# A hybrid decoder trunk in float32: the first half layer's conditioning is made in four column groups, with the first projection pass worked between them

## The reference

```python
cond = jax.nn.silu(c)
for l in range(DEPTH):
    ada = (cond @ w_ada[l] + b_ada[l])[:, None, :]
    sh_m, sc_m, g_m, sh_f, sc_f, g_f = jnp.split(ada, N_ADA, axis=-1)
    h = x * (1.0 + sc_m) + sh_m
    y = hybrid_mixer(h, ...)                      # h @ w_in (2048 x 6672), three head groups, @ w_out
    x = layer_norm(DEEPNORM_ALPHA * x + (1.0 + g_m) * y, ln_g[l, 0], ln_b[l, 0])
    h = x * (1.0 + sc_f) + sh_f
    y = jnp.square(jax.nn.relu(h @ w1[l])) @ w2[l]
    x = layer_norm(DEEPNORM_ALPHA * x + (1.0 + g_f) * y, ln_g[l, 1], ln_b[l, 1])
```

## Time and profile before

| | |
|---|---|
| median of 3 runs | 2568.55 us (2568.52 to 2571.52) |
| the profiled execution's own time | 2575.91 us |
| its span, first to last instruction | 2574.1 us |
| mean granted TensorE clock | 0.986 |
| TensorE busy with matmuls | 2431.5 us, 94% of the span |
| VectorE busy | 1912.3 us, 74% |
| ScalarE busy | 1167.5 us, 45% |
| loaded from memory | 629.5 MB, 245 GB/s over the span |
| TensorE's first unit | starts at 109.87 us |
| end of pass 0 | 160.9 us |

### The profile page before, as it was taken

One profiled execution on the slowest core, in us unless ns is written; L12 is line 12 of the kernel. 1 busy time (PEld: TensorE's weight loads), 2 busy tenths in 40 slices (PEclk: granted clock), 3 DMA queues, 4 the chain that ended last, 5 costly groups with the idle time before them and its releaser, 6 DMA issues.

```text
span 2574.1 us, 36539 instructions
## 1 busy us (share of the span) xinstructions
PE 2431.5 (94%) x14932; PEld 2181.3 (85%) x14932; DVE 1912.3 (74%) x2008; ACT 1167.5 (45%) x1511; POOL 268.0 (10%) x148
## 2 busy tenths in 40 slices
PE   2499998999999999999999999999999999999997
PEld 2498986878989989989988898787898998998986
DVE  6889897788988787787877568768898555555556
ACT  0264473654443533534436446555444353343442
POOL 0001251010011011011010013301001101101101
PEclk9999998999999999999999999999999999999998
DMA  9898566886888888898875635578788656656653
GB/s 390 337 334 288 173 216 204 283 313 244 286 311 329 283 306 302 298 315 297 295 234 171 172 93 168 186 262 301 256 284 294 202 185 192 188 185 192 185 189 109
DMA packets 176075, 634.01 MB, mean 246 GB/s; under 512 B 20188, under 2 KB 20772, under 8 KB 174500
## 3 DMA queue, kind: packets, MB, share of 16 engines
q1 hardware_dynamic: 171648, 614.80, 70.7%
q0 software_dynamic: 2576, 14.68, 1.5%
q10 hardware_dynamic: 1684, 2.19, 0.2%
HBM read 629.50 MB, written 2.10 MB: 245 GB/s over the span
## 4 chain that ended last, share of the span: by engine, by line
PE 83%; DVE 8%; DMA 6%; issue 3%; ACT 1%; ACTq 0%; DVEq 0%
PE PB L1520 40%; PE PB L1529 28%; PE PB L1488 7%; DMA ADR<-in_w_ada 3%; DVE ACC L949 2%; DVE WL L1036 1%; PE PB L1502 1%; DMA RAW<-in_w_ada 1%; PE PB L1426 1%; PE PB L1558 1%; PE PB L1473 1%; DMA RAW<-in_w_in 1%; PE PB L1433 1%; DVE SM L1238 0%; DMA ST<-in_ln_b 0%
## 5 line engine op out<-in xcount | busy, mean ns | idle before, releaser
L1036 DVE TENSOR_TENSOR WL<-RAW,WH 128x1024 fp32r<-128x1024 f32 (+1 forms) x800 | 1010.9, 1270 | 491.4 <-ACT WH L670 490.5
L670 ACT ACTIVATE WH<-RAW 128x1024 fp32r<-128x1024 f32 (+1 forms) x800 | 833.0, 1044 | 1118.5 <-PE PB L1520 567.0
L1529 PE MATMUL PB<-HTh,WH 128*128 128x256 f32 x2176 | 619.9, 285 | 0.0
L1529 PE MATMUL PB<-HTh,WL 128*128 128x256 f32 x2176 | 615.8, 283 | 0.0
L1529 PE MATMUL PB<-HTl,WH 128*128 128x256 f32 x2176 | 615.7, 283 | 0.0
L949 DVE SCALAR_TENSOR_TENSOR ACC<-ADR,CT,ACC 128x1024 f32<-128x1024 f32 x300 | 409.8, 1366 | 54.5 <-DMA ADR<-in_w_ada 52.7
L1529 PEld LDWEIGHTS PB<-HTh,WH 128*128 128x128 f32 x2176 | 417.6, 192 | 0.8 <-issue 0.5
L1529 PEld LDWEIGHTS PB<-HTl,WH 128*128 128x128 f32 x2176 | 417.6, 192 | 0.8 <-issue 0.5
L1529 PEld LDWEIGHTS PB<-HTh,WL 128*128 128x128 f32 x2176 | 417.4, 192 | 0.0
L1520 PE MATMUL PB<-WH,T2h 128*128 128x512 f32 x1208 | 378.2, 394 | 7.4 <-DVE T2l L1042 7.4
L1520 PE MATMUL PB<-WL,T2h 128*128 128x512 f32 x1208 | 374.5, 391 | 0.0
(11 more groups left out here) (282 smaller groups left out, 2197.3 us busy)
## 6 DMA issues: line engine op xcount, KB each, us to landing
RAW<-in_w SPq DMA_DIRECT2D x512, 512.0 KB, 4.6
ADR<-in_w_ada SPq DMA_DIRECT2D x320, 512.0 KB, 5.2
RAW<-in_w_in SPq DMA_DIRECT2D x192, 512.0 KB, 3.8
RAW<-in_w_ada SPq DMA_DIRECT2D x64, 512.0 KB, 15.9
RAW<-in_w_out SPq DMA_DIRECT2D x64, 512.0 KB, 6.3
RAW<-in_w_in SPq DMA_DIRECT2D x32, 264.0 KB, 2.8
GB<-in_b_ada POOLq DMA_DIRECT2D x8, 512.0 KB, 7.5
LNG<-in_ln_g POOLq DMA_DIRECT2D x4, 1024.0 KB, 7.1
```

The lines of the kernel that those rows point to most:

```text
L670: act.activation(WH[:, wh_slot(layer, n), 0:w], RAW[:, k, 0:w], ACT.Copy).then_inc(hi_done.sem, 1)
L1036: tt(WL[:, k, 0:w], RAW[:, k, 0:w], WH[:, wh_slot(layer, n), 0:w].bitcast(F32), ALU.subtract).then_inc(lo_done.sem, 1)
L1529: ins = mm(dst, w[:, slot[w is WL], cols], a[:, kt, :], start=first and i == 0 and j % 2 == 0, stop=last and i == 2, skip_group_check=True)
```

## The change

The shift and scale of the first half layer are made in four groups c_ = 0 to 3 of 512 columns each, instead of four blocks q of 1024. A block of group c_ holds 512 columns of the shift and the 512 of the scale that belong to the same four tiles of h (two pieces of 2,048 bytes in each of its 128 rows). After each group the four units of pass 0 that read its tiles are worked, while the next group is made. Blocks 2, 6, 10 and 14 of each group are multiplied on TensorE (`pro_direct`, 8 matmuls of one column each), the other 12 on VectorE (`pro_part`), so that VectorE has 48 macs instead of 64. The landing slots are eight (RAW2); RAW is used for the units from the start. c and the identity are loaded first; the silu comes from a transpose of its own. The loads of LMs and of two parts of K move to GpSimd's queue after the last mac of group 3, and the copy to LM to position (1, 12). The plan of the first layer's later blocks moves: block 6 starts at 16 instead of 0, and blocks 8, 9, 4 and 5 take 74 to 138.

```diff
-PRO_SLOTS = 16
+PRO_SLOTS = 8
+DIRECT = (2, 6, 10, 14)
...
-ADA_PLAN = [[(6, 0, 18), (7, 19, 34), (8, 35, 50), (9, 75, 92), (4, 93, 114), (5, 115, 137),
+ADA_PLAN = [[(6, 16, 34), (7, 35, 50), (8, 74, 92), (9, 93, 106), (4, 107, 124), (5, 125, 138),
              (10, 144, 168), (11, 169, 195), (12, 196, 218), (13, 219, 248), (14, 249, 266),
...
-            for a in range(64):
+            def pro_load(c, k):
+
+                dst, arrived, _ = pro_in_slot(c, k)
+                a = 16 * c + k
                 if a >= PRO_SLOTS:
-                    sp.wait_ge(ada_mac.sem, a - PRO_SLOTS + 3)
-                dst, arrived = pro_slot(a)
-                sp.dma_start(dst, w_ada_r[(a % 16) * P:(a % 16 + 1) * P, (a // 16) * UW:(a // 16 + 1) * UW]
+                    sp.wait_ge(*pro_used(*divmod(a - PRO_SLOTS, 16)))
+                src = w_ada_r[k * P:(k + 1) * P, 0:2 * D].rearrange("p (s n) -> p s n", s=2)
+                sp.dma_start(dst.rearrange("p (s n) -> p s n", s=2), src[:, :, c * 512:(c + 1) * 512]
                              ).then_inc(arrived, 16)
+
+            for c_ in range(4):
+                for k in range(8):
+                    pro_load(c_, k)
+                for kt in range(4 * c_, 4 * c_ + 4):
+                    raw_load(0, kt, w_in_r[ds(kt * P, P), COL0[0]:COL0[0] + UW])
+                for k in range(8, 16):
+                    pro_load(c_, k)
...
+            pool.wait_ge(pro_mac.sem, pro_macs(3, 15))
+            for dst, src in ((LMs[:, :], consts[:, K_LM:K_LM + 1024]), (K[:, K_ML:K_TRI], consts[:, K_ML:K_TRI]),
+                             (K[:, K_DG:K_KEEP], consts[:, K_DG:K_KEEP])):
+                pool.dma_start(dst, src).then_inc(pro_k.sem, 16)
...
+            for dst, src in ((CS[:, :], c.rearrange("b (t p) -> (b t) p", p=P)), (K[:, 0:P], consts[:, 0:P])):
+                act.dma_start(dst, src).then_inc(pro_c.sem, 16)
+            for dst, src in first:
                 act.dma_start(dst, src).then_inc(pro_st.sem, 16)
+            act.wait_ge(pro_cT.sem, 1)
+            act.activation(E16[:, :], PB[0][:, 0:KT], ACT.Exp, scale=-1.0).then_inc(pro_act.sem, 1)
...
-            for n in range(W_SLOTS):
+            for c_ in range(4):
+                for n in range(4 * c_, 4 * c_ + 4):
+                    hi_split(0, n)
+                h_tiles(0, 0, 2 * c_)
+                h_tiles(0, 0, 2 * c_ + 1)
+            for n in range(KT, KT + AHEAD):
                 hi_split(0, n)
...
+            for c_ in range(4):
+                for k in range(16):
+                    if k not in DIRECT:
+                        pro_part(c_, k)
+                    if k >= 11 and k < 15:
+                        lo_split(0, 4 * c_ + k - 11)
+                    if (c_, k) == (0, 9):
+                        tables()
+                    if (c_, k) == (1, 3):
+                        tables_end()
+                        layer_cols(0)
+                pro_cols(c_)
+                h_lo(0, 0, 2 * c_)
+                h_lo(0, 0, 2 * c_ + 1)
+            for n in range(KT, KT + AHEAD):
                 lo_split(0, n)
...
+            pro_direct(0, 2)
+            pro_direct(0, 6)
+            x_transpose(0, 0, 0)
+            x_transpose(0, 0, 1)
+            pro_direct(0, 10)
+            pro_direct(0, 14)
+            for c_ in range(4):
+                pro_sums(c_)
+                if c_ < 3:
+                    pro_direct(c_ + 1, 2)
+                for j in range(4):
+                    n = 4 * c_ + j
+                    first_unit(0, 0, n, 0, n, n == 0, n == KT - 1)
+                    if c_ < 3 and j in (0, 2):
+                        x_transpose(0, 0, 2 * c_ + 2 + j // 2)
+                    if c_ < 3 and j == 1:
+                        pro_direct(c_ + 1, 6)
+                if c_ < 3:
+                    pro_direct(c_ + 1, 10)
+                    pro_direct(c_ + 1, 14)
```

More of the change, by code:

```diff
@@ L269, in hybrid_trunk @@
         hT_ready = Signal("hT_ready", 32)
-        cols_set = Signal("cols_set", 2)
+        cols_set = Signal("cols_set", 2, 3)
         t2_T = Signal("t2_T", 3)
@@ L395, in work, with h_bank, sums_at @@
             return PB[4 * (1 - p % 2) + b]
+        def h_bank(layer, s, b):
+            return work(s * FF0, b % 4 if layer or s else b % 3)
         def is_gate(q):
             return q % 12 // 2 in (2, 5)
+        def sums_at(q):
+            return ADA_POS[q] - 3
         def cols_at(layer, q):
-            return ADA_POS[12 * layer + q] + 1
+            return sums_at(12 * layer + q)
         def ada_arrived(a):
@@ L681, in h_tiles @@
             def h_tiles(layer, s, b):
-                if b == 0:
+                first = layer == 0 and s == 0
+                if first:
+                    act.wait_ge(cols_set.sem, b // 2 + 1)
+                elif b == 0:
                     act.wait_ge(cols_set.sem, cols_set.at(layer, s + 1))
@@ L687, in h_tiles @@
                     kt = 2 * b + j
-                    cols = work(s * FF0, b % 4)[:, j * SEQ:(j + 1) * SEQ]
+                    cols = h_bank(layer, s, b)[:, j * SEQ:(j + 1) * SEQ]
                     bias, scale = SH[:, s, kt:kt + 1], SC[:, s, kt:kt + 1]
@@ L1251, in _ @@
                         at = (p, kt)
-                        if (layer or n + AHEAD >= W_SLOTS) and n + AHEAD < FF0 * KT + 2:
+                        if n + AHEAD < FF0 * KT + 2:
                             lo_split(layer, n + AHEAD)
@@ L1262, in _ @@
                             conditioning_out(q, p, ada_bank(n - 2))
+                        if at == (1, 12) and layer == 0:
+                            dve.wait_ge(pro_k.sem, 16 * 3)
+                            link(dve.tensor_copy(LM[:, :], LMs[:, :]))
                         if at == (1, 3):
@@ L1463, in _, with pro_direct @@
-            pe.wait_ge(ada_cols.sem, 4)
+            def pro_direct(c_, k):
+                block_, arrived, count = pro_in_slot(c_, k)
+                if k == DIRECT[0]:
+                    if c_:
+                        pe.wait_ge(cols_set.sem, c_)
+                    else:
+                        pe.wait_ge(pro_ct.sem, 1)
+                pe.wait_ge(arrived, count)
+                for i in range(8):
+                    ins = mm(PB[7][:, i:i + 1], block_[:, i * P:(i + 1) * P], CT[:, k:k + 1],
+                             start=k == DIRECT[0] and i == 0, stop=False, skip_group_check=True)
+                ins.then_inc(pro_dir.sem, 1)
@@ L1465, in x_transpose, with pro_sums @@
+            def pro_sums(c_):
+                if c_ == 0:
+                    pe.wait_ge(pro_in.sem, 16 * 6)
+                pe.wait_ge(pro_mac.sem, pro_macs(c_, 15))
+                for i in range(8):
+                    ins = mm(PB[7][:, i:i + 1], PACC[c_ % 2][:, i * P:(i + 1) * P], ones, start=False, stop=True,
+                             skip_group_check=True)
+                ins.then_inc(pro_sum.sem, 1)
             def x_transpose(layer, s, b):
-                if b >= 4:
-                    pe.wait_ge(hT_tx.sem, hT_tx.at(layer, 16 * s + 2 * (b - 4) + 2))
+                ring = 4 if layer or s else 3
+                if b >= ring:
+                    pe.wait_ge(hT_tx.sem, hT_tx.at(layer, 16 * s + 2 * (b - ring) + 2))
@@ L1624, in _ @@
                                 pe.wait_ge(hg_log.sem, hg_log.at(layer, 1))
+                                if layer == 0 and p == 2:
+                                    pe.wait_ge(pro_k.sem, 16 * 3)
                             if i in (0, 4):
```

182 lines of the change are left out of this document (87 added, 95 removed).

## The result

The change makes the kernel slower: 2581.08 us (median of 4 runs, 2577.97 to 2582.83) against 2570.03 (4 runs, 2568.52 to 2572.11). The ratio is 1.0037, 95% interval 1.0024 to 1.0049: +11 us where -11 was forecast. The profiled execution of the changed kernel took 2582.83 us with a span of 2581.0, 6.9 us more than the span of before; its mean clock is 0.976 instead of 0.986. The other 4 us lie between the profiled executions and the medians (the profile of before lies 5.9 us above its median, that of after 1.7).

What follows compares the result with a forecast made beforehand. Memory was taken to bound the start, then TensorE after pass 0, with two waits for VectorE. The terms -19, -3.4 and +11.5 gave -11 us, so 2557.5 us; 8-in-10 range 2543 to 2569.

Steps and rivals of the forecast that it cites:

- part 3: Plan positions 93 to 138, where 48 macs stand instead of 32: +11.5 us (4 to 18).
- part 1: End of pass 0, made in groups: ends at 142 us instead of 160.9, -19 us (-29 to -12).
- I take the larger: Sums of block 5: of 45.3 us by two-slot turns and 43.4 by VectorE's time, the larger; stall 7 us.
- Block 4 has 17 positions and costs nothing beyond that: Block 4's macs, positions 107 to 124: no cost beyond block 9's 2.3 us (0 to 6).
- The sums are as many as before: Positions 93 to 138: the number of sums on TensorE is unchanged, so no time was added for them.
- 21.2 us, and it fits: TensorE's own turn of a group in pass 0, at full clock, against 27.4 us of DMA and VectorE's 26.9.
- 149: Late bound for the end of pass 0, in us, if TensorE's clock falls between groups and loads come late: -12.
- Part 2: Plan up to position 92: one mac fewer before VectorE reaches MW, -3.4 us (0 to -4).
- one mac less on that path: Block 8 has no mac at position 82, where one takes 3.42 us ahead of MW: -3.4 us.
- The late constants and the copy of LM: Around pass 1: 4 us of loads and a 0.7 us copy, hidden under TensorE's work, so no cost.
- paid back: Rival: pass 0 ends at 149 and positions 93 to 138 cost 16 us; no change, 2569 us; chance 0.13.
- low-clock rival: Rival: TensorE stays at low clock in pass 0, turns 41.6 us, 2608; chance 0.09, shared with 7.5 us mac turns.

## Why the prediction was wrong

The sum had -19, -3.4 and +11.5. The traces have -11.0, -2.7 and +20.1, and +0.5 behind. The larger miss is part 3. Neither turns the sign by itself: with only part 1 wrong the sum is -2.9, with only part 3 wrong -2.3; together they give the +6.4 at which the last four units begin.

**Part 3, mis-sized: "I take the larger".** The mechanism was right: the wait appeared at the sums of block 5, with VectorE waiting for ADR. Its size came from two limits, 45.3 us by the turns of two slots and 43.4 by VectorE's own time, of which the larger was taken. The larger is not the answer, for each limit was worked out as if the other cost nothing. The chain shows stretches of load and mac in turn (540 to 556, 566 to 584 us) and between them a stretch in which VectorE does other work (556 to 566) and the loads wait for it. The first turn itself was shorter than forecast, 4.21 + 1.30 = 5.5 us instead of 6.18; from the first mac to the last it took 49.6 us all the same. Without loads it took 43.8 from the start of one sums to the start of the other, 1.7 of them for the first sums themselves; VectorE's limit had been put at 43.4. Stall: 10.2 us, forecast 7.

**"Block 4 has 17 positions and costs nothing beyond that"** failed: the wait for T2l, which stands behind blocks 9 and 4, grew by 4.0 us, and in the run with the plan on the kernel before by 5.5. The forecast had 2.3 us for block 9 and none here. The clock was allowed 1.5 us; behind the stall the sums took 3.75 us instead of 1.72 and the unit 3.51 instead of 2.74, 2.8 us, and the five units behind T2l 16.04 instead of 13.7. The 2.3 us of these are not new, for behind its own wait for T2l the kernel before lost 51.92 - 18 x 2.74 = 2.6 us as well. "The sums are as many as before" failed too: from position 93 on stand the sums of three blocks (9, 4 and 5) instead of two, 1.8 us. So the 20.1 us are 10.2, 4.0, 2.8 and 1.8, and 1.3 that these rows do not place.

**Part 1, failed at the turns: TensorE's "21.2 us, and it fits" and VectorE's 26.9.** TensorE's was worked out "if the clock is full". In the turn from 102.62 us the sums and the first direct block took 3.57 us each instead of 1.75, and the first unit 4.6 instead of 2.88: 5.4 us more. In the turn before, the last pair of direct blocks took 4.89 instead of 3.63 us as well, and there TensorE stood for nothing but the columns: its list took the whole 28.5 us. The low clock was in the text as the bound of the range ("149", which is where pass 0 ended) and as a rival, not in the sum. VectorE's own turn, from 102.56 to 131.42 us, was 28.9 us, of which 0.9 was a wait for DMA. The 28.0 left are 1.1 more than forecast: 1.4 for macs that stand 1.39 apart and not 1.2, less 0.4 for standing. The 3.5 us of sums at the low clock were in its forecast already. Line by line: the last mac of group 0 came 1.8 us late, three turns took 87.1 instead of 82.8 us, the stretch behind the last mac 18.4 instead of 16.7 (its first unit ran at the low clock): 7.8 of the 8 us.

The third limit, DMA's 27.4 us a turn, was near: 20 blocks at 392 GB/s are 26.7, and pieces of 2 KB cost about the 0.09 us that the sum had for them. But with 4 KB pieces pass 0 ended only 1.2 us sooner, against 6 us in the forecast's sum of the landings. The forecast set turns of 26.9, 27.4 and 21.2 us side by side and went by VectorE's. The real ones were 28.0, 26.7 and 27 to 28.5, each engine waits for the others at two or three points of a turn, and with eight slots the turn was 29.05. No run changes the clock alone (the one with more matmuls adds work too), so what the low clock by itself cost pass 0 stays open; making TensorE's list shorter by other means brought 0.9 us.

**Part 2 was right in its number (-2.7 for -3.4) by luck.** The wait for MW did shrink, to 7.3 us for "near 8". But "one mac less on that path" gave nothing: the mac moved to a place ahead of SB, the wait of 2.9 us ahead of pass 5 came with it, and the lead stayed at 13.7 us from 342.7 us on. The 2.7 us had come earlier: TensorE has the sums of two blocks instead of three between pass 0 and MW, 1.8 us (those that part 3 has too many), and a wait for SM was 0.6 us shorter (0.2 instead of 0.8). The forecast also took the wait for MW as a matter of GpSimd and the count of macs alone. In the kernel before a third slot takes 7 us from it, for the loads made VectorE late before GpSimd began; in the changed kernel the wait stays at 7.2 us with three slots, but comes 4 us sooner.

The reading of the busy line was off in one place: of the first two slices only the first has DMA at nine tenths or more, the second reads 8, since pass 0 begins in it. Nothing in the sum hangs on it.

**The late constants and the copy of LM** cost nothing that shows in the traces, as forecast.

Of the rivals, "paid back" named the right pair (pass 0 at 149, part 3 at 16) and came nearest; it was 4 us short in part 3. The gate rule of the Trainium skill (TensorE: Matmul & The Clock Gate, "What's actually happening") stood beside the low-clock rival: full speed is what activity releases. The traces agree in part: a granted clock of 0.50 and 0.56 in stretches that begin with a group's sums, then full speed within the first unit, but also the low clock where TensorE had hardly stood. It cost some 6 to 7 us a turn of TensorE, not the 20 of the full rival (41.6 less 21.2). Since VectorE and memory had turns nearly as long, that rival's 2608 was far off.

## What to carry to other kernels

Where two limits of one chain take turns (a load that needs a slot, an engine that is busy elsewhere), the time is above the larger of the two (49.6 us here, for limits of 45.3 and 43.4); give one slot more, or leave the loads out, to see which it is, and look at the kernel before with the same eyes: one more slot was worth 7.5 us there, about as much as everything else here. Work moved in a plan must be costed at the density of where it lands and at every wait of TensorE in that range, not only the last: one mac moved eight positions forward shortened the wait for MW and brought one for SB, and nothing was gained. Compare the two traces at several landmarks, for a step whose total is right may be made of errors that cancel. A stage in which three engines have turns within 2 us of each other has no single bound: shortening one alone gave 1 us here, three more landing slots gave 5, and the longest turn is a lower bound of what is measured, not a forecast.

## What was not expected of the hardware

A TensorE that is busy is not thereby at full clock: with sums and direct blocks of one-column products it was busy 11.68 of 12 us at a granted clock of 0.56, and six matmuls of 256 columns ahead of the sums brought these from 3.57 to 1.92 us. Macs that each wait for the one directly before stand 1.39 us apart, those that wait for the one before that 1.20. Loads of 512 KB in pieces of 2,048 bytes, with one in five in pieces of 4,096, ran at 392 GB/s at share 1.03; with all in pieces of 4,096 the same stretch of the same list ran at 412 at the same share, 5% more.
